# Token-shift sums of r, k and v made in DRAM by accumulating transfers, and a new order of the recurrence's jobs

## The reference, cut to what matters

```python
z = h @ W_in                      # columns: q | k | v of attention, then zr | zk | zv, 512 each
def token_shift(z):
    return jnp.pad(z, ((0, 0), (1, 0), (0, 0)))[:, :-1]      # row t becomes row t+1
r = zr + (token_shift(zr) - zr) * mu_rkv[0]
k = zk + (token_shift(zk) - zk) * mu_rkv[1]
v = zv + (token_shift(zv) - zv) * mu_rkv[2]
...
kk = k * k_k
kk = kk * lax.rsqrt(jnp.maximum(jnp.sum(kk * kk, axis=-1, keepdims=True), 1e-24))   # per head
k = k * (1.0 + (a - 1.0) * k_a)
y = rwkv7_scan(r, decay, k, v, -kk, kk * a)    # S <- S diag(w) + (S a) b^T + v k^T;  y = S r
```

## Time and profile before

| | us |
|---|---|
| time, median of 3 runs | 3442.6 (3440.2 to 3445.67) |
| span of the profiled execution | 3425.3 |
| PE busy | 3019.8 (88%) |
| DVE busy | 2072.7 (61%) |
| ACT busy | 1574.2 (46%) |
| POOL busy | 792.0 (23%) |

### The profile page before, as it was taken

The page is one execution under the profiler, slowest core; times in us unless marked ns, Lnnn a source line. Parts: engine busy times, 40 slices in busy tenths (PEclk is TensorE's granted clock), DMA queues, the critical chain, the costliest instruction groups (busy, mean ns, idle before and its releaser), DMA issues. The chain is left out here.

```text
span 3425.3 us, 69307 instructions
## 1 busy us (share of the span) xinstructions
PE 3019.8 (88%) x25224; PEld 2433.3 (71%) x25224; DVE 2072.7 (61%) x3031; ACT 1574.2 (46%) x2560; POOL 792.0 (23%) x1065
## 2 busy tenths in 40 slices
PE   7999999996898858888887699399999999995899
PEld 5776887884666637777776588378787787874787
DVE  4443772225777754555554333679898898985565
ACT  3332211004777744343343211078787787875232
POOL 1000330002133145666654100000000100001443
PEclk9999999998999978999999899599999999997999
DMA  5555347546000022112110665445968777774343
GB/s 174 183 181 193 130 157 261 195 180 168 7 12 13 7 80 83 64 64 89 70 64 19 213 213 202 187 153 207 359 264 327 299 281 284 269 293 153 122 144 110
DMA packets 237483, 554.35 MB, mean 162 GB/s; under 512 B 27008, under 2 KB 62976, under 8 KB 229024
## 3 DMA queue, kind: packets, MB, share of 16 engines
q1 hardware_dynamic: 218896, 484.07, 39.6%
q0 software_dynamic: 11552, 41.95, 3.4%
q10 hardware_dynamic: 6768, 24.64, 1.8%
HBM read 408.52 MB, written 142.09 MB: 161 GB/s over the span
## 5 line engine op out<-in xcount | busy, mean ns | idle before, releaser
L583 PE MATMUL p_z<-w_in_part,hn_split 128*128 128x512 f32 x2304 | 536.1, 393 | 9.0 <-DMA hn_split<-s_hT 4.5
L583 PEld LDWEIGHTS p_z<-w_in_part,hn_split 128*128 128x128 f32 x2304 | 433.4, 189 | 99.7 <-DMA hn_split<-s_hT 5.3
L1711 DVE TENSOR_TENSOR e_w_part<-w_gate_up_sb,e_w_part 128x1024 fp32r<-128x1024 f32 x380 | 452.8, 1221 | 58.4 <-ACT e_w_part L1706 56.7
L1706 ACT CAST e_w_part<-w_gate_up_sb 128x1024 fp32r x380 | 396.9, 1052 | 160.7 <-PE pe_gate L2472 73.4
L2472 PE MATMUL pe_gate<-e_w_part,e_xT 128*128 128x512 f32 x1128 | 286.8, 412 | 26.3 <-DVE e_w_part L1711 26.3
L2484 PE MATMUL pe_y<-e_w_part,e_hT 128*128 128x512 f32 x1128 | 276.2, 401 | 13.2 <-DVE e_w_part L1711 13.2
L2472 PEld LDWEIGHTS pe_gate<-e_w_part,e_xT 128*128 128x128 f32 x1128 | 217.7, 196 | 77.9 <-issue 21.3
L2472 PE MATMUL pe_up<-e_w_part,e_xT 128*128 128x512 f32 x1128 | 271.0, 396 | 0.0
L1711 DVE TENSOR_TENSOR e_w_part<-w_down_sb,e_w_part 128x1024 fp32r<-128x1024 f32 x188 | 218.1, 1220 | 62.2 <-ACT e_w_part L1706 61.9
L2484 PEld LDWEIGHTS pe_y<-e_w_part,e_hT 128*128 128x128 f32 x1128 | 209.8, 189 | 60.6 <-DVE e_w_part L1711 13.6
L2472 PEld LDWEIGHTS pe_up<-e_w_part,e_xT 128*128 128x128 f32 x1128 | 211.9, 188 | 51.3
(11 more groups left out here) (424 smaller groups left out, 5625.5 us busy)
## 6 DMA issues: line engine op xcount, KB each, us to landing
w_gate_up_sb<-in_w_gate_dram SPq DMA_DIRECT2D x32, 2048.0 KB, 12.9
w_gate_up_sb<-in_w_up_dram SPq DMA_DIRECT2D x32, 2048.0 KB, 19.4
w_down_sb<-in_w_down_dram SPq DMA_DIRECT2D x32, 2048.0 KB, 9.0
hn_split<-s_hT SPq DMA_DIRECT2D x48, 1024.0 KB, 5.3
s_y<-e_y ACTq DMA_DIRECT2D x47, 512.0 KB
s_hT<-hn_split SPq DMA_DIRECT2D x16, 1024.0 KB, 6.6
s_y<-d_zeros SPq DMA_DIRECT2D x16, 1024.0 KB, 6.4
s_zn<-z_stage SPq DMA_DIRECT2D x48, 256.0 KB, 2.0
```

Source lines behind the costliest of these rows:

```text
L583: last = nc.tensor.matmul(bank, hs[m % 3][:, a, k, :].bitcast(F32R), w_part(c, b)[:, k, :].bitcast(F32R), start=(k == 0 and a == b == 0), ...
L1706: return nc.scalar.copy(high, src)
L1711: return nc.vector.tensor_tensor(low, src, high, ALU.subtract)
```

## The change

There is one DRAM tensor `s_z` in the place of `s_zr` and `s_zn`. SP stores only the past tile, one row lower. POOL issues a second transfer for the now tile, with `accum_op=ALU.add`, which adds it to what `s_z` holds (`add_now`). It waits until the past tiles of this and of the preceding row tile have landed, until all earlier adds have landed (semaphore `added`), and until the stage is filled. In pass 0 the add of tile i - 1 follows the reciprocal root of tile i in POOL's program. The stage of a now tile comes free when its add has landed.

In the recurrence the sums are loaded ready: r and k into `rk_` (512 KB), v straight into `V` (256 KB, semaphore `v_in`). POOL's three adds and ACT's copy are gone. V of the next tile and then rk, sig and a of the tile after it are issued once Y0 of this tile is done; the store of the result and the load of g stay at `out`. The orders of PE, ACT, DVE and POOL change: on ACT `sqk` stands behind X2 and `Pex` behind Y0; on DVE `ssk` stands behind MN, `kkn` behind S0, `yc` before TX4, `bon` before TX5; on POOL `Rh` comes first and `T_init` before `Kh`.

```diff
+    SUMMED = {STAGED[(name, i)] for name in MIXED for i in range(TILES)}
...
+        def landed(n):
+
+            if n in SUMMED:
+                return added, 16 * sum(m <= n for m in SUMMED)
+            return out_dma[n % Z_STAGES], 16 * sum(m not in SUMMED for m in range(n % Z_STAGES, n + 1, Z_STAGES))
+
         def wait_free_stage(eng, key):
             n = STAGED[key]
             if n >= Z_STAGES:
-                eng.wait_ge(out_dma[n % Z_STAGES], 16 * (n // Z_STAGES))
+                eng.wait_ge(*landed(n - Z_STAGES))
...
-                    now = t["zn"] if name in MIXED else t["zr"][1:SEQ + 1, :]
-                    dst = now[rows, c * BANK:(c + 1) * BANK]
+                    dst = t["z"][i * P + 1:(i + 1) * P + 1, c * BANK:(c + 1) * BANK]
...
-                store(("zr", i))
                 store(("zr_past", i))
...
-                for name in ("zk", "zk_past", "zv", "zv_past"):
+                for name in ("zk_past", "zv_past"):
...
+            def add_now(name, i):
+
+                now = STAGED[(name, i)]
+                cols = slice(MIXED.index(name) * BANK, (MIXED.index(name) + 1) * BANK)
+                for row in range(max(i - 1, 0), i + 1):
+                    pool.wait_ge(*landed(STAGED[(name + "_past", row)]))
+                if STAGED[(name, i)] > min(SUMMED):
+                    pool.wait_ge(added, 16 * sum(m < now for m in SUMMED))
+                pool.wait_ge(staged[now % Z_STAGES], now // Z_STAGES + 1)
+                pool.dma_start(t["z"][i * P:(i + 1) * P, cols], stage[now % Z_STAGES][:], accum_op=ALU.add).then_inc(added, 16)
             for i in range(TILES):
                 pool.wait_ge(ss_done, i + 1)
                 rsqrt(rstd[:, i % 2:i % 2 + 1], ss[:, i % 2:i % 2 + 1], 0).then_inc(rstd_done, 1)
                 pool.drain()
+                if i >= 1:
+                    add_now("zr", i - 1)
+            add_now("zr", TILES - 1)
             for i in range(TILES):
                 pool.wait_ge(qss_done, i + 1)
                 rsqrt(qrs[:], qss[:], 1).then_inc(qrs_done, 1)
                 pool.drain()
+            for i in range(TILES):
+                add_now("zk", i)
+                add_now("zv", i)
...
-ACT_EV = ["P", "cumsb", "Tr0", "X1a", "X1b", "Wa", "sqk", "Wb", "Tr1", "X2a", "X2b", "Pex", "Tr2", "X3a", "X3b", "Y0",
-          "Tr3", "X4a", "X4b", "D", "sqy", "pc", "vcopy", "Tr4", "X5a", "X5b", "T0", "T1", "T2", "T3", "Tr5"]
-DVE_EV = ["G3a", "G3b", "G1a", "G1b", "TX1a", "TX1b", "kp", "ssk", "G2a", "G2b", "TX2a", "TX2b", "MN0", "MN1", "kkn", "RT0", "RT1", "TX3a", "TX3b",
-          "S0", "S1", "Ya", "Yb", "TX4a", "TX4b", "s1", "yc", "Ah", "Bh", "s2", "TX5a", "TX5b", "bon", "yn"]
-POOL_EV = ["kk0", "rkv", "rsk", "ex", "b", "Kh", "Rh", "rk", "T_init", "rsy", "bv", "out"]
+ACT_EV = ["P", "cumsb", "Tr0", "X1a", "X1b", "Tr1", "Wa", "Wb", "X2a", "X2b", "sqk", "Tr2", "X3a", "X3b", "Y0", "Pex",
+          "Tr3", "X4a", "X4b", "sqy", "pc", "D", "Tr4", "X5a", "X5b", "T0", "T1", "T2", "T3", "Tr5"]
+DVE_EV = ["G3a", "G3b", "G1a", "G1b", "TX1a", "TX1b", "kp", "G2a", "G2b", "TX2a", "TX2b", "MN0", "MN1", "ssk", "RT0", "RT1", "S0", "kkn",
+          "TX3a", "TX3b", "S1", "Ya", "Yb", "s1", "yc", "TX4a", "TX4b", "Ah", "Bh", "s2", "bon", "TX5a", "TX5b", "yn"]
+POOL_EV = ["Rh", "kk0", "rsk", "ex", "b", "T_init", "Kh", "rk", "rsy", "bv", "out"]
...
+            def load_v(i, s):
+                sp.dma_start(V[s][:], t["z"][i * P:(i + 1) * P, 2 * RW:3 * RW]).then_inc(v_in[s], 16)
+            for i in range(2):
+                load(i, i)
+            for i in range(2):
+                load_v(i, i)
...
+            def reload(i, s):
+                sp.wait_ge(PO.sem, PO.value("rk", i - 1))
+                sp.wait_ge(AC.sem, AC.value("pc", i - 1))
+                load(i + 2, s)
...
+                    sp.wait_ge(PE.sem, PE.value("Y0", i))
+                    load_v(i + 1, (i + 1) % 2)
+                if i + 1 < TILES - 1:
+                    reload(i, i % 2)
+                finished(i, i % 2)
...
-                    pool.wait_ge(z_in[n], nth(i + 1, j, 1) * 64 + 64)
-                    pool.tensor_tensor(rkv[n][:, k_], rkv[n][:, k_], z[n][:, k_], ALU.add)
-                    pool.drain()
-                ev("kk0", mul(kk0[:], rkv[n][:, k_], k_k[:]))
-                if real:
-                    pool.tensor_tensor(rkv[n][:, r_], rkv[n][:, r_], z[n][:, r_], ALU.add)
-                ev("rkv", mul(rkv[n][:, v_], rkv[n][:, v_], z[n][:, v_], ALU.add))
-                pool.drain()
+                    pool.wait_ge(z_in[n], nth(i + 1, j, 1) * 48 + 48)
+                    pool.wait_ge(AC.sem, AC.value("P", i))
+                ev("Rh", mul(Rh[:], rk_[n][:, r_], Pt[:]))
+                ev("kk0", mul(kk0[:], rk_[n][:, k_], k_k[:]))
...
-                ev("vcopy", lambda: nc.scalar.copy(V[n][:], rkv[n][:, 2 * RW:3 * RW]), (PO, "rkv"), (PE, "Y0"))
...
-                level(1); w_("a"); filled(1); w_("b")
-                level(2); g12("G2", 3); filled(2); two_jobs(("MN0", "MN1"), mn, (AC, "Wb", 0))
-                level(3); two_jobs(("RT0", "RT1"), rt); filled(3); each("Y0", range(HV), y0); s_(0)
-                level(4); s_(1); two_jobs(("Ya", "Yb"), y_, (DV, "RT1", 0), (DV, "S0", 0)); filled(4)
-                chunked("D", range(HV), d_, (DV, "G2b", 0), (AC, "vcopy", 1)); job("pc", chunk_ends)
+                level(1); filled(1); w_("a")
+                tr(1); w_("b"); x_(2, "a"); x_(2, "b"); g12("G2", 3); filled(2); two_jobs(("MN0", "MN1"), mn, (AC, "Wb", 0))
+                tr(2); s_(0); two_jobs(("RT0", "RT1"), rt); x_(3, "a"); x_(3, "b"); each("Y0", range(HV), y0); filled(3); s_(1)
+                tr(3); two_jobs(("Ya", "Yb"), y_, (DV, "RT1", 0), (DV, "S0", 0)); x_(4, "a"); x_(4, "b"); job("pc", chunk_ends); filled(4)
+                if "main" in what:
+                    pe.wait_ge(v_in[s], i // 2 * 16 + 16)
+                chunked("D", range(HV), d_, (DV, "G2b", 0))
```

More of the change, by code:

```diff
@@ L121, in phase_project @@
         z_done = sem("A_z"); ev_act = sem("A_evac_act"); ev_dve = sem("A_evac_dve")
-        staged = [sem(f"A_staged{s}") for s in range(Z_STAGES)]; out_dma = [sem(f"A_out{s}") for s in range(Z_STAGES)]
+        staged = [sem(f"A_staged{s}") for s in range(Z_STAGES)]; out_dma = [sem(f"A_out{s}") for s in range(Z_STAGES)]; added = t["lasting"].enter_context(nc.semaphore("A_added"))
         s_pos = sem("A_positions"); s_ang = sem("A_angles"); s_trig = sem("A_trig")
@@ L257, in _ @@
                     load_h(3 * TILES + i + 2)
-                for name in ("zk", "zk_past", "zv", "zv_past"):
+                for name in ("zk_past", "zv_past"):
                     store((name, i))
             for s in range(Z_STAGES):
-                sp.wait_ge(out_dma[s], 16 * sum(n % Z_STAGES == s for n in STAGED.values()))
+                sp.wait_ge(out_dma[s], 16 * sum(n % Z_STAGES == s and n not in SUMMED for n in STAGED.values()))
+            sp.wait_ge(added, 16 * len(SUMMED))
             sp.wait_ge(qT_out, 16 * TILES)
@@ L1071, in phase_rwkv @@
         two = lambda n, s, d=F32: [sb(f"{n}{k}", s, d) for k in range(2)]
-        z = two("c_z", [P, 3 * RW]); rkv = two("c_rkv", [P, 3 * RW])
+        rk_ = two("c_rkv", [P, 2 * RW])
         sig = two("c_sig", [P, RW]); a = two("c_a", [P, RW]); g = two("c_g", [P, RW])
@@ L1136, in load @@
             def load(i, s):
[L1137 to L1142 removed]
+                rows = slice(i * P, (i + 1) * P)
+                sp.dma_start(rk_[s][:], t["z"][rows, 0:2 * RW]).then_inc(z_in[s], 16)
+                sp.dma_start(sig[s][:], t["lo"][0, rows, :]).then_inc(z_in[s], 16)
+                sp.dma_start(a[s][:], t["lo"][1, rows, :]).then_inc(z_in[s], 16)
+            def load_v(i, s):
[4 more added lines that the diff above has]
+                load_v(i, i)
             sp.sem_inc(o_out, 16)
@@ L1331, in step @@
                 evac("Y0", Y0[:])
+                ev("Pex", lambda: nc.scalar.activation(Pex[:], cumsb[:], ACT.Exp, scale=-DECAY), (PO, "ex"))
                 tr(3)
@@ L1427, in step @@
                     ev(f"MN{c}", mn, (PE, f"MN{c}"))
-                ev("kkn", lambda: nc.vector.tensor_tensor(heads(kkn[:]), heads(kk0[:]), rsk[:].unsqueeze(2).broadcast_to([P, HV, DH]), ALU.mult),
-                   (PO, "rsk"))
+                if "prep" in what:
+                    dve.wait_ge(AC.sem, AC.value("sqk", i))
+                    nc.vector.tensor_reduce(ssk[:], heads(sq[:]), AX.X, ALU.add)
+                    dve.drain()
+                ev("ssk", lambda: nc.vector.tensor_scalar(ssk[:], ssk[:], 1e-24, None, ALU.max))
                 for c, r in enumerate(CHUNKS):
```

117 lines of the change are left out of this document (47 added, 70 removed), and 8 rows, old and new, of the table PE_JOBS.

## The result

| | us |
|---|---|
| before, 4 runs | 3441.4 (3438.37 to 3445.67) |
| changed, 4 runs | 3483.8 (3471.34 to 3490.8) |
| ratio | 1.0122 (95% interval 1.0104 to 1.0141) |

The change makes the kernel 1.2% slower. The forecast was 3430, with 3392 to 3466 as its range. The profiled execution of the changed kernel took 3481.29 with a span of 3479.6. So only 1.7 us lie around a span. The 17.3 us that the prediction put there for the kernel before were something else: with the same 1.7 its profiled execution took 3427, a fast one, 14 to 15 us under the median.

The account below looks back on a forecast made before the run. PE was taken to bound projection pass 0 (busy 277.75 of 279.00 us), with some 8 us a tile to gain in the recurrence. Projection +29.3 and recurrence -41.3 gave -12: 3442.6 to 3430, range 3392 to 3466.

Parts of the forecast that it names:

- the projection's +29.3: Projection: 21.6 us from ACT waiting for the stage in pass 0, 5 for PE's clock, 2.7 at the end; bounds 3 and some 80.
- R1: Rival, slower: an accumulate in pass 0 lands as slowly as a gather's median, 4.9 us; +11 in all, 3453.6; chance 0.17.
- In passes 1 to 3 the adds are off every path: Projection, passes 1 to 3: adds of zk and zv cost nothing, since a stage there is refilled several us later.
- +2.7: End of the projection: a whole add follows the last store's landing before the next phase, +2.7 us (1.0 to 4.1).
- The recurrence's -41.3: Recurrence: -2.7 us a tile, -38 for 14 tiles, and -3.5 at the start; bounds 0 and about -75.
- The five rows that I named: Recurrence: PE's issue waits at five source lines, 35.2 us or 2.7 a tile; 1.9 of it goes with smaller load bursts.
- the T jobs' 6.2 us of waits: Recurrence: PE's T jobs wait 0.5 us a tile for last inputs; three additions less give -0.4, bounds 0 and -0.5.
- The +0.8 for W: Recurrence: W's first half moves behind TX1 and no longer covers X1's evacuation; +0.8 us a tile, bounds 0 and +1.0.
- The clock: Recurrence: with half the idle time gone, a quarter of the 2.2 us the clock costs returns; -0.6 a tile.
- At the start: Recurrence, tile 0: waits for 1.0 MB of loads in place of 2.0 and loses POOL's first addition; -3.5 us.
- R3: Rival, slower: kkn and yc on DVE, beside POOL's products, take +1.0 and +0.8 us a tile; 3456; chance 0.13.
- R4: Rival, faster: an accumulate costs little more than a store, landing in 2.6 us; projection about 11, time 3412; chance 0.10.

## Why the prediction was wrong

- **The step that failed is the projection's +29.3: it measured +77.8**, in three places. That is 48 of the 54 us by which 3430 missed the median.
  - In pass 0, forecast 26.6, measured 52.2 up to its last product. The landing time of an accumulate, L: 3.6 assumed, 4.7 measured. Three quarters of a gather's median was a guess by bytes; the median itself, 4.9, was the nearer row. With the add issued 0.4 later behind the past tile than I had it, ACT was late by 4.66, exactly the figure of R1, and R1's 38.6 for the tiles and 11 for the clock stand against the 52.2 (27 us of pass 0 ran at 1.2 GHz, which loses up to 14; 3 before the change). R1 is what happened in pass 0, at a chance of 0.17. That its figure fits to the second decimal is luck: it had 0.2 too much for L and 0.4 too little ahead of it.
  - "In passes 1 to 3 the adds are off every path": wrong. I asked when a stage is refilled and not how many adds a single chain can make. One per 5.5 was needed and one per 5.9 was made, in pass 3 with a mean landing of 5.0 and 0.9 from one landing to the next issue. A chain like that ends with what it has fallen behind: +20.1 where I had +2.7.
  - The start of pass 1 came 4.5 later still (PE waits 9.0 for h in place of 4.5); I had nothing there. The passes between make up the last 1.0.
- R1 lacked the second of these too: its +11 became +42.
- The drain: not foreseen. In the changed kernel it hardly shows, since ACT's wait comes first; with that taken away it held 16 us.
- **The recurrence's -41.3 was -25.6 between the two traces**, some -35 by the medians, and -37 to -40 by itself with the experts' part allowed for. How much it fell short by is open: six traces of the same changed recurrence take 614 to 637 us from the first to the last instruction on its tiles (the three with full sums 619 to 637), and before the change there is one, of 646. Term by term in the two traces:
  - The waits for instructions beside bursts fell by (31.7 - 6.6) / 14 = 1.8 a tile and rose by 0.4 outside, together -1.4 where I took -1.9. The five rows that I named fell from 35.2 to 17.9 where I forecast about 10, and others rose. The reading of the earlier trace rows held: PE waited for its own instructions.
  - ACT no longer waits for kk0 ahead of X's evacuation, and the T jobs' 6.2 us of waits are 0.4, both as forecast. The +0.8 for W was wrong in kind: the wait for c_X came, but undoing it gave nothing.
  - The clock gave back 0.15 a tile where I had 0.6: PE's busy time went from 31.04 to 30.89.
  - At the start 0.9 was gained, not 3.5: before the first `cum` PE waits 22.9 us in place of 24.6, but the first tile then takes 1.2 longer. Some 4 us were gained behind the last `cum`, where I had nothing.
  - The period of a tile went from 36.8 to 35.3 (14 tiles), and over the 12 tiles of the earlier trace rows by 1.9, against 2.7.
- R3: kkn was stretched by 1.07 us, and yc by 0.08 where R3 had 0.8. The two instructions of kp shrank by 1.0 and 0.9, since POOL's adds beside them are gone; R3 left that out. So DVE lost nothing in sum, and R3's price is not tested. The Trainium skill (page "SBUF — State Buffer", section "Who interferes with whom") says that a VectorE instruction with two SBUF inputs contends with a GpSimd instruction that reads SBUF. Both groups agree, and so do kkn at 692 ns and kp at 1615 once POOL's product had moved from the one to the other.
- R4's L of 2.6 is excluded: the quickest add took 4.0 in the changed kernel, and even a plain transfer by POOL 3.1 in the median. The prediction also prices this L twice, at about 14 and at about 11. The time around the span was misread as well; it shifted the forecast by nothing, since only differences were used.

Open: why the place of a burst and PE's order matter beside the size; how much of the loss by long bursts is the clock's (it was not tried to hold it fixed); and what makes the same recurrence differ by 24 us from one execution to another.

## What to carry to other kernels

Before a plain store becomes an accumulate behind another store, add up the whole chain that now holds the buffer (landing, issue, landing) and compare it with the slack of whoever refills it; then compare the number of such transfers per stretch with how many a single chain can make while the loads of that stretch run. Give the buffer its own place, keep the transfer away from drains on its engine, and let transfers on different rows go by semaphores of their own. Count the bytes that load beside a large unrolled program: its instructions come as DMA packets too, and PE waited longer for them beside loads. Look in the trace whether an edit took a collision away or only moved it. And when an experiment leaves out part of a computation, compare the phases behind it first: here the experts' part alone became up to 20 us longer.

## What the runs showed of the hardware

- An accumulate of 256 KB from SBUF to DRAM, issued by POOL, lands in 4.0 to 7.5 us, 4.7 in the median (changed kernel); six that went out just ahead of a load of 1 MB took 6.9 to 7.5. A plain transfer on the same queue lands in 2.3 to 5.1, median 3.1; SP's in 2.0 in the median.
- A drain on POOL waits for POOL's own transfer in flight and ends 0.08 us after its landing (22 of 22 drains, with landings from 3.1 to 6.6): up to 4402 ns in place of 312.
- PE's instructions are fetched in packets of 16 KB, one for 256 to 257 recorded instructions, one per 5.6 us in the recurrence (85 in 480). Where PE stood idle for over 0.7 us at one, it was 2.1 us in a burst of loads (31.7 in 15) and 1.1 outside (11.8 in 11). 768 KB a tile more of loads cost 27 us by the ratios and 32 by the medians.
- A VectorE instruction of 128x512 f32 with two inputs from SBUF took 679 to 692 ns alone and 1600 to 1749 beside POOL's work on such tiles.
